# Value tiles of the first block's heads projected with tokens on partitions

## What is computed

```python
p = h @ w_in[l]
q_a, k_a, v_a, o_a, i_a, f_a, q_b, k_b, v_b, g_a, g_b = jnp.split(p, split_idx, axis=-1)
qk_a = jax.nn.silu(causal_conv(jnp.concatenate([q_a, k_a], axis=-1), conv_w[l]))
...
h_a = mlstm_chunkwise(q_a, k_a, v_a, i_pre, f_pre)         # branch a
y_a = jax.nn.sigmoid(o_a) * head_rms_norm(h_a, mlstm_norm_g[l])
y_b = stick_breaking(qn, kn, v_b)                          # branch b
gates = jax.nn.sigmoid(jnp.concatenate([g_a, g_b], axis=-1) + b_gate[l])
y = gates[..., :D_MODEL] * y_a + gates[..., D_MODEL:] * y_b
x = x + y @ w_out[l]
```

## Time and profile before

| | before |
|---|---|
| median of 3 runs | 1409.86 us (1407.19 to 1410.21) |
| the profiled execution | 1410.33 us; 1408.6 us of it is the span of the trace |
| PE busy | 1331.4 us, 95% of the span |
| weight loads (PEld) | 1066.5 us, 76% |
| VectorE, ScalarE, GpSimd | 50%, 45%, 9% |
| mean granted clock of TensorE | 0.977 of full speed |

### The profile page before, as it was taken

One profiled execution on the slowest core, in us unless ns is written; L12 is line 12 of the kernel. 1 busy time (PEld: TensorE's weight loads), 2 busy tenths in 40 slices (PEclk: granted clock), 3 DMA queues, 4 the chain that ended last, 5 costly groups with the idle time before them and its releaser, 6 DMA issues.

```text
span 1408.6 us, 16618 instructions
## 1 busy us (share of the span) xinstructions
PE 1331.4 (95%) x6008; PEld 1066.5 (76%) x6008; DVE 701.6 (50%) x1161; ACT 638.7 (45%) x927; POOL 124.8 (9%) x232
## 2 busy tenths in 40 slices
PE   4799999999999998999999999999878999999699
PEld 3677878777787776788888888878646777777577
DVE  5344443454444443452443424453798887443661
ACT  5455564555635561441332313353725454554540
POOL 1010100101000010000000000000112111140230
PEclk9899999999999999999999999999978999999899
DMA  5312122222222213123222322241111323535511
GB/s 204 105 64 89 53 89 76 84 67 67 97 67 93 67 63 140 69 94 116 89 89 92 111 95 89 94 170 69 60 60 55 118 97 102 205 102 188 209 60 60
DMA packets 26608, 138.05 MB, mean 98 GB/s; under 512 B 3400, under 2 KB 3464, under 8 KB 13520
## 3 DMA queue, kind: packets, MB, share of 16 engines
q1 hardware_dynamic: 15792, 109.06, 22.3%
q0 software_dynamic: 5168, 18.08, 3.9%
q10 hardware_dynamic: 5616, 10.49, 2.0%
HBM read 123.97 MB, written 12.60 MB: 97 GB/s over the span
## 4 chain that ended last, share of the span: by engine, by line
PE 89%; DVE 5%; ACT 3%; DMA 2%; issue 1%; ACTq 0%; POOL 0%; DVEq 0%; POOLq 0%
PE proj L288 72%; DMA x_res<-in_x 2%; PE pa L1288 2%; PE pm L1247 1%; PE pm L1295 1%; PE pm L1404 1%; PE pa L1254 1%; PE pa L1404 1%; PE pa L1247 1%; PE pa L1386 1%; PE pm L1386 1%; PE pa L1265 1%; PE pm L1396 1%; DVE rope L1034 1%; PE pm L1274 1%
## 5 line engine op out<-in xcount | busy, mean ns | idle before, releaser
L288 PE MATMUL proj<-h_hi,w_hi 128*128 128x512 f32 x1040 | 419.3, 403 | 17.7 <-DVE h_lo L1190 11.0
L288 PE MATMUL proj<-h_lo,w_hi 128*128 128x512 f32 x1040 | 407.7, 392 | 0.0
L288 PE MATMUL proj<-h_hi,w_lo 128*128 128x512 f32 x1040 | 407.6, 392 | 0.0
L261 DVE TENSOR_TENSOR w_lo<-w_raw,w_hi 128x2048 fp32r<-128x2048 f32 x102 | 234.3, 2309 | 172.6 <-ACT w_hi L255 170.0
L255 ACT ACTIVATE w_hi<-w_raw 128x2048 fp32r<-128x2048 f32 x102 | 193.4, 1911 | 159.0 <-PE proj L288 147.1
L288 PEld LDWEIGHTS proj<-h_hi,w_hi 128*128 128x128 f32 x1040 | 197.1, 189 | 65.2 <-issue 18.2
L288 PEld LDWEIGHTS proj<-h_hi,w_lo 128*128 128x128 f32 x1040 | 196.8, 189 | 42.3
L288 PEld LDWEIGHTS proj<-h_lo,w_hi 128*128 128x128 f32 x1040 | 197.3, 190 | 41.5 <-issue 2.9
L288 PE MATMUL proj<-w_hi,act_hi 128*128 128x512 f32 x256 | 99.6, 389 | 0.0
L288 PE MATMUL proj<-w_hi,act_lo 128*128 128x512 f32 x256 | 99.6, 389 | 0.0
L288 PE MATMUL proj<-w_lo,act_hi 128*128 128x512 f32 x256 | 99.6, 389 | 0.0
(11 more groups left out here) (354 smaller groups left out, 1865.3 us busy)
## 6 DMA issues: line engine op xcount, KB each, us to landing
w_raw<-in_wall SPq DMA_DIRECT2D x102, 1024.0 KB, 5.1
gates<-gate_st ACTq DMA_DIRECT2D x24, 256.0 KB, 2.0
m_all<-gates POOLq DMA_DIRECT2D x1, 2560.0 KB, 12.2
x_res<-in_x ACTq DMA_DIRECT2D x4, 512.0 KB, 11.7
bc<-gate_rows POOLq DMA_DIRECT2D x8, 256.0 KB, 3.4
x_res<-in_x POOLq DMA_DIRECT2D x1, 2048.0 KB, 11.7
x<-x_res POOLq DMA_DIRECT2D x1, 2048.0 KB, 7.1
heads_out<-o_st ACTq DMA_DIRECT2D x8, 256.0 KB, 2.0
```

The source lines that it names most:

```text
L261: nc.vector.tensor_tensor(w_lo[:, slot, 4 * half:4 * half + 4, :], w_raw[:, half], w_hi[:, slot, 4 * half:4 * half + 4, :], ALU.subtract)\
L288: mm = nc.tensor.matmul(proj[:, bank, :], lhsT, rhs, start=(k == 0 and q == 0), stop=(k == kts - 1 and q == 2))
```

## The change

Both value tiles of a head are projected by a new function, with the activations as the stationary operand (128 tokens at a time) and 256 weight columns, `v_b` and `v_a` side by side, moving. Two groups of 128 tokens share a PSUM bank. The result already has tokens on partitions and is copied to one buffer, `v_ba`. The transposes, their PSUM use, the copies out of `pm` and the semaphores `v_turned` and `v_sb` are gone. The weight columns change places: the first group of a head now ends with g_b, the second is v_b, v_a, o_a, g_a. So tile 3 is g_b, tiles 4 and 5 are the values (tokens 0 to 255, then 256 to 511), 6 is o_a and 7 is g_a. The gate of branch b is now the one with an early copy, and the gate of branch a is made from PSUM at the end.

```diff
+        v_ba = at("v_ba", 81 * K, [P, TB, 512])
+        def project_v(g, slot, n, bank, ts):
+            nc.tensor.wait_ge(S["tile_free"], n - 1)
+            for t in ts:
+                c = slice(t * P, (t + 1) * P)
+                for k in range(KT):
+                    if k % 4 == 0:
+                        nc.tensor.wait_ge(S["w_lo_done"], 2 * g + 1 + k // 4)
+                    for q, (w, a) in enumerate(((w_hi, h_hi), (w_hi, h_lo), (w_lo, h_hi))):
+                        mm = nc.tensor.matmul(proj[:, bank, 256 * (t % 2):256 * (t % 2 + 1)], a[:, k, c],
+                                              w[:, slot, k, 0:256], start=(k == 0 and q == 0),
+                                              stop=(k == KT - 1 and q == 2))
+            return mm
...
                 a.wait_ge(S["tile_made"], n + 4)
-                a.activation(v_bT[:, :], proj[:, 1], ACT.Copy).then_inc(S["tile_free"], 1)
+                a.activation(gate_b[:, :], proj[:, 1], ACT.Copy).then_inc(S["tile_free"], 1)
...
                 a.wait_ge(S["tile_made"], n + 5)
-                a.activation(v_aT[:, :], proj[:, 0], ACT.Copy).then_inc(S["tile_free"], 1)
+                a.activation(v_ba[:, 0:2, 0:2 * P], proj[:, 0].rearrange("p (t n) -> p t n", t=2), ACT.Copy)\
+                    .then_inc(S["tile_free"], 1)
...
-                a.wait_ge(S["v_turned"], h + 1)
-                a.activation(v_b[:, :], pm[:, 0:512], ACT.Copy).then_inc(S["v_sb"], 1)
-                a.activation(v_a[:, :, 0:P], pm[:, 512:1024].rearrange("p (t n) -> p t n", t=TB), ACT.Copy).then_inc(S["v_sb"], 1)
                 split_hi(ga + 2, 1, 1)
                 a.wait_ge(S["tile_made"], n + 6)
-                a.activation(gate_o[:, :], proj[:, 1], ACT.Copy).then_inc(S["tile_free"], 1)
+                a.activation(v_ba[:, 2:4, 0:2 * P], proj[:, 1].rearrange("p (t n) -> p t n", t=2), ACT.Copy)\
+                    .then_inc(S["tile_free"], 1)
...
                 a.wait_ge(S["tile_made"], n + 7)
-                a.activation(gate_a[:, :], proj[:, 0], ACT.Copy).then_inc(S["tile_free"], 1)
+                a.activation(gate_o[:, :], proj[:, 0], ACT.Copy).then_inc(S["tile_free"], 1)
...
-                a.activation(gate_a[:, :], gate_a[:, :], ACT.Sigmoid, bias=par[:, 5:6]).then_inc(S["gate_sig"], 1)
+                a.activation(gate_b[:, :], gate_b[:, :], ACT.Sigmoid, bias=par[:, 6:7]).then_inc(S["gate_sig"], 1)
                 a.wait_ge(S["tile_made"], n + 8)
-                a.activation(gate_b[:, :], proj[:, 1], ACT.Sigmoid, bias=par[:, 6:7]).then_inc(S["tile_free"], 1)
+                a.activation(gate_a[:, :], proj[:, 1], ACT.Sigmoid, bias=par[:, 5:6]).then_inc(S["tile_free"], 1)
...
-                v.wait_ge(S["gate_sig"], 2 * h + 2)
+                v.wait_ge(S["tile_free"], T_HEADS + 8 * h + 8)
                 v.wait_ge(S["y"], 4 * h + 1)
                 v.tensor_tensor(scl[:, :], scl[:, :], gate_a[:, :], ALU.mult).then_inc(S["y"], 1)
                 v.wait_ge(S["pv_b_made"], h + 1)
-                v.wait_ge(S["tile_free"], T_HEADS + 8 * h + 8)
+                v.wait_ge(S["gate_sig"], 2 * h + 2)
...
-                tile(4)
-                t_.wait_ge(S["tile_free"], n + 5)
+                made(project_v(ga + 1, 0, n + 4, 0, (0, 1)))
+                made(project_v(ga + 1, 0, n + 5, 1, (2, 3)))
                 t_.wait_ge(S["a_col"], 2)
-                for m, vT in enumerate((v_bT, v_aT)):
-                    for i in range(TB):
-                        mm = t_.transpose(pm[:, 512 * m + P * i:512 * m + P * (i + 1)], vT[:, P * i:P * (i + 1)], ident[:, :])
-                mm.then_inc(S["v_turned"], 1)
-                tile(5)
-                t_.wait_ge(S["v_sb"], 2 * h + 2)
                 t_.wait_ge(S["ka_landed"], 16 * h + 16)
                 triangle(pm, k_a, silu, DQK_A).then_inc(S["s_made"], 1)
...
                 t_.wait_ge(S["p_masked"], 4 * h + 4)
+                t_.wait_ge(S["tile_free"], n + 6)
```

More of the change, by code:

```diff
@@ L132, in program @@
         bc = at("bc", 57 * K, [P, SEQ])
-        names = "q_b k_b sq_q sq_k conv silu k_a v_bT v_aT v_b gate_o gate_a gate_b".split()
-        (q_b, k_b, sq_q, sq_k, conv, silu, k_a, v_bT, v_aT, v_b, gate_o, gate_a, gate_b) = [
+        names = "q_b k_b sq_q sq_k conv silu k_a gate_o gate_a gate_b".split()
+        (q_b, k_b, sq_q, sq_k, conv, silu, k_a, gate_o, gate_a, gate_b) = [
             at(n, (61 + 2 * i) * K, [P, SEQ]) for i, n in enumerate(names)]
-        v_a = at("v_a", 87 * K, [P, TB, P + 1])
+        v_ba = at("v_ba", 81 * K, [P, TB, 512])
         y_tok, scl = sq_k, silu
@@ L378, in _ @@
             gp.memset(eps[:, :], EPS).then_inc(S["consts"], 1)
-            gp.memset(v_a[:, :, P:P + 1], 1.0).then_inc(S["consts"], 1)
+            gp.memset(v_ba[:, :, 2 * P:2 * P + 1], 1.0).then_inc(S["consts"], 1)
             gp.memset(one_row[:, :], 1.0).then_inc(S["consts"], 1)
@@ L1294, in _ @@
                         o = TRI[i] + P * (t - i)
-                        mm = t_.matmul(by_tok[:, t // 2, t % 2, :], decay[:, o:o + P], v_a[:, i, :],
+                        mm = t_.matmul(by_tok[:, t // 2, t % 2, :], decay[:, o:o + P], v_ba[:, i, P:2 * P + 1],
                                        start=(i == 0), stop=(i == t))
@@ L1303, in _ @@
                 t_.wait_ge(S["a_b"], h + 1)
-                weighted(pa[:, 0:512], lambda i: v_b[:, P * i:P * (i + 1)], z).then_inc(S["pv_b_made"], 1)
+                weighted(pa[:, 0:512], lambda i: v_ba[:, i, 0:P], z).then_inc(S["pv_b_made"], 1)
             t_.wait_ge(S["head_done"], HEADS)
@@ L1456, in lay_out @@
         wall[G_HEADS + 2 * h] = np.concatenate(
-            [q_b[:, :, wide], k_b[:, :, wide], q_a[:, :, narrow], k_a[:, :, narrow], v_b[:, :, wide]], axis=2)
-        wall[G_HEADS + 2 * h + 1] = np.concatenate([w[:, :, wide] for w in (v_a, o_a, g_a, g_b)], axis=2)
+            [q_b[:, :, wide], k_b[:, :, wide], q_a[:, :, narrow], k_a[:, :, narrow], g_b[:, :, wide]], axis=2)
+        wall[G_HEADS + 2 * h + 1] = np.concatenate([w[:, :, wide] for w in (v_b, v_a, o_a, g_a)], axis=2)
     for j in range(2):
```

## The result

The changed kernel takes 1417.05 us (median of 7 runs, 1412.85 to 1419.43), the kernel before beside it 1408.47 us: a ratio of 1.0058, with a 95% interval of 1.0045 to 1.0072. It is slower by 8.6 us, or 0.6%, where 0.4 us and at most 0.3% had been forecast. The profiled execution took 1416.94 us, 1415.2 of it the span; the kernel before had 1408.6.

The account below looks back on a forecast made before the run. PE was taken as the bound, busy 95% of the span. Per head -0.23 (slack saved) + 0.28 (longer tile 4) = +0.05 us, +0.4 over eight heads: 1410.7, said as 1410.3 us; range 1407.3 to 1414.

Parts of the forecast that it names:

- part 1: Transposes between tiles 4 and 5 go: 1.69 us per head off PE's order, but only 0.23 gained, as `k_a` binds.
- `k_a`'s slack: Time `k_a` lay ready before PE loaded it at the triangle: 0.18 to 0.28 us, taken as 0.23, bounds 0 and 0.28.
- The gates' new order and the copies: ACT's copies and the last sigmoid before DVE's product with `gate_a`: cost nothing, cover about 10 and 0.3 us.
- Part 3: Tile 5 takes 5.8 us in place of 5.5, hidden behind `k_a`; a PE wait of about 1.3 us is left per head.
- rival (b): Each head's wait before the triangle lets PE's clock fall, 1.5 us a fall; all eight heads 1422 us; 7%.
- the 1.54 us that passed: PE wait at 932.71 with no clock fall behind it, held against the clock falling at the shorter new wait.
- the bounds of the slope and the slack: Per 256-column matmul 0.113 to 0.125 us, tile 4 -0.04 to +0.51 us; `k_a` lying ready 0 to 0.28 us.

Follow-up runs that it names:

- e2_rows128: The changed kernel with branch a's triangle made over 128 rows in place of 64, zeros in `k_a`: 1408.33 us.
- e10_late_ka_rows128: The kernel before with `k_a` delayed by fourteen small GpSimd operations and the triangle over 128 rows: 1418.76 us.
- e4_late_copy: The changed kernel with ScalarE's copy of the first value tile moved behind the sigmoid, so `k_a` no longer waits for that tile: 1398.17 us.

## Why the prediction was wrong

The steps of the sum held as far as PE's order and its wait go. The value tiles' matmuls start 0.12 us apart; the load of `k_a` stands 12.96 us behind tile 4's first matmul, where 12.91 + 0.05 was foretold; PE idles for 1.20 us where about 1.3 was; a head without a fall takes 59.58 us where about 59.6 was. Of part 1 only `k_a`'s slack is saved, and it is the 0.23 us I took: from POOL's issue to the load are 2.43 us before (85.29 to 87.72) and 2.20 in the changed kernel (84.66 to 86.86), with the same 2.1 to 2.2 to the landing. The load stood 0.28 us behind the landing before, and 0.04 in the changed kernel. So the DMA that the list of waits names in the earlier trace rows was not what PE waited for; in the changed kernel it is. The gates' new order and the copies cost nothing visible.

The step that failed is Part 3: the wait of 1.3 us left in each head was taken at its length alone, and what it does to the clock was put at nothing in the sum. It cost six falls, 9.6 us, and made 1417.05 us of what had been 1408.47. The fall of the clock stood only in rival (b), to which I gave 7%. There its mechanism was named, its price of a fall (1.5 us; 1.6 measured) and the point from which it decides (two falls) were right, and it is what happened, with six falls where it had reckoned eight. What was wrong is its weight, by one comparison: "my wait is shorter than the 1.54 us that passed". I compared waits by their length alone. The wait that passed was followed by transposes of full height; the one in the head is followed by a triangle of half height, a difference which stands in the rows themselves (64*128 in the earlier trace rows). e2_rows128 and e10_late_ka_rows128 show that this decides at waits of 1.2 and 1.4 us.

The Trainium skill, page "TensorE: Matmul & The Clock Gate", section "HAM oscillation", tells of a kernel in which waits for a DMA between bursts of matmuls brought the clock down each time. The waits that it tells of are longer than mine, so it did not foretell these falls: here 1.20 us were enough. It also speaks of the wait only, and with full height behind it the same wait passed in all eight heads.

The range, 1407.3 to 1414, reached for the bounds of the slope and the slack, which hardly moved, and stopped short of the one rival with a price of 12 us.

The gain went, then, in two steps. The transposes' 1.69 us per head turned into 0.58 for the matmuls of both tiles (last one starts 11.48 us behind the first, 12.59 before) and 1.16 more between the last of them and the load of `k_a` (1.48, 0.32 before), 0.05 too much; and the wait turned into falls of the clock. e4_late_copy shows that both are undone by making `k_a` earlier: the head is then 1.20 us shorter than before (59.54 to 58.34).

## What to carry to other kernels

Taking work off the bound engine pays only as far as the next thing it waits for was already there: look for it before the cut, and move its chain forward in the same change (here one copy on an engine that idled 1.4 us in front of it). A new wait on TensorE of about 1 us is not only its own length: read what stands behind it, and reckon 1.6 us for each fall of the clock. Where a matmul of few rows stands between full ones, padding it with zeros costs nothing in columns, and here it saved 0.4 us a head without a wait, 0.2 with one, and kept the clock up behind waits of 1.2 and 1.4 us. How far this goes is open: behind one of the two waits of 2.42 us the clock fell at full height too.

## What the runs showed of the hardware

- A wait of 0.73 to 1.5 us on TensorE followed by a matmul burst of half height made the clock fall in two to six heads of eight; a wait of 1.2 or 1.4 us followed by the same matmuls at full height did so in none of sixteen. The lower clock shows 1.2 to 2.7 us behind the start of those matmuls, in the last of them or in the next tile, and costs 1.6 us each time, or twice that. Full height is no full cover: one wait of 2.42 us of two was followed by a fall.
- A load of 64 rows behind matmuls of 128 is not made under them, nor one of 128 behind 64: 0.40 us for the pair of switches around the triangle with nothing to hide it (58.34 to 57.94 us a head), 0.38 in the kernel before. The Trainium skill, page "TensorE: Matmul & The Clock Gate", section "The mechanism", has loads overlap with running matmuls when their row groups differ or when they go to the background weight buffer; here loads of equal height overlap, and those of another height, which share rows with the matmul that runs, do not.
- A float32r matmul of 256 columns with its own weights costs 0.120 us in a run of 96, one of 512 0.227. The Trainium skill, page "TensorE: Matmul & The Clock Gate", section "Back-to-back issue gap", gives 262 and 518 cycles, an estimate of 109 and 216 ns at 2.4 GHz, by which two of 256 would cost 0.003 us more than one of 512; measured are 0.013.
